# Summing gathered expert rows four tokens at a time instead of two, in a one-core layer with product-key experts

## The chip, the cores and the metric

The program runs on one core of one Trainium2 chip. The metric is the device time of one execution in microseconds (us), lower is better. The number to compare is the median over several executions.

## What is computed

One layer of a streaming encoder is applied to 1024 frames of a new stream (eight blocks of 128 tokens) and to 64 frames of a running one (a ninth block, called SAMPLE). Attention and retention come first and lead to `x1`; they matter here only as work that runs beside. The second half is a layer of 16384 single-neuron experts. Every token picks 128 of them (8 heads, 16 each) and computes

```
q = (xblk @ w_q).reshape(PEER_BLOCK, PEER_HEADS, 2, PEER_HALF)
...
u = u_table[expert]
hid = jax.nn.gelu(jnp.einsum('thkd,td->thk', u, xblk).astype(jnp.float32), approximate=False)
v = v_table[expert]
return jnp.einsum('thk,thkd->td', (g * hid).astype(xblk.dtype), v)
```

Both tables have rows of 1024 float32, so a token needs 128 rows of 4 KB from `u_table` and 128 from `v_table`. For 1088 tokens that is 1.14 GB of gathered rows.

## The kernel before

A **gather** is one indirect DMA of 128 rows (512 KB), issued by GpSimd (POOL in the profile) at L618. A u gather fetches one expert for each of the 128 tokens of a block; VectorE (DVE, L865) multiplies it with the tokens and adds up along the row. A v gather fetches the 128 experts of one token; TensorE (PE, L1195) sums them, weighted, into that token's row of the result. Both kinds land in one ring of `RING = 10` tiles, strictly in one order. POOL works through this order too: the gather that is number `n` waits until the tile of number `n - 10` has been read.

For the v tiles TensorE uses weights of 32 columns: `spread` holds, for each token, a 128x32 matrix with the token's weights in one column and zeros elsewhere. The product lands in one of four groups of 32 partitions of the accumulator, and `v_token` deals the tokens so that four successive v tiles go to the four groups in turn. A tile of 1024 columns takes two matmuls of 512 (`c` is 0 or 1), and a float32 matmul shows as two records in the profile. The v tiles are summed in pairs: the function `pair` waits for both tiles, issues four matmuls, and raises the semaphore `summed` once.

`seg_items` writes down the order. A segment `(u, v)` interleaves the u gathers of one block with the v gathers of an earlier one. After `LEAD = 8` u items come two v items, two u items, two v items and so on. Segment (8,7) has only 64 u gathers (the SAMPLE block is packed into half the slots), so there it is two v, one u. Segments (None,0) and (None,8) are v alone. The segments are grouped in `PHASES`; in each phase a pair of blocks goes through its dense work (projections, attention, output, query product, the search for the experts called the peer step). The class `Threader` places the ring items between the dense steps: before each dense step an engine first works off all items up to a slot that `Pace` gives. Each engine does this by itself in its program order, so a v item that TensorE has reached holds up its dense steps until the tiles have landed, and a u item does the same on VectorE. The last phase has no dense work: segments (7,6), (8,7) and (None,8).

The weights of the dense products come in pieces of 1 MB through the queue of SyncE (L501).

Of the kernel before, what the change touches and what calls it, by code (L numbers as in the profile page):

```python
# [27 lines left out]
P = 128  # L28
# [34 lines left out]
VBUF = 5  # L63
# [6 lines left out]
def rows(b):  # L70

    return CHUNK if b == SAMPLE else P


def u_slots(b):

    return SLOTS // 2 if b == SAMPLE else SLOTS


def u_before(b):  # L80
    return SLOTS * b


def v_before(b):
    return P * b


def v_token(b, i):

    groups = rows(b) // 32  # L90
    return 32 * (i % groups) + i // groups
# [14 lines left out]
def place(b):  # L106

    return 2 if b == 0 else next(blocks.index(b) for blocks, _ in PHASES if b in blocks)
# [4 lines left out]
    return [c for c in range(b + 1) if place(c) == place(b)]  # L113


PAIR = 2
LEAD = 8


def v_pairs(b):  # L120
    return rows(b) // PAIR


def pairs_before(b):
    return P * b // PAIR


def seg_items(prev, seg):


    u, v = seg
    us = [("u", u, k) for k in range(u_slots(u))] if u is not None else []
    vs = [("v", v, k) for k in range(rows(v))] if v is not None else []
    lead = LEAD if us else 0
    items = [("load", u, 0)] * bool(us) + us[:lead // 2]
    if prev[0] is not None:
        items.append(("spread", prev[0], 0))
    items += us[lead // 2:lead]
    if prev[1] is not None:
        items.append(("final", prev[1], 0))  # L140
    if not vs:
        return items + us[lead:] + [("weights", u, 0)]
    at, n = lead, len(vs) // PAIR
    for q in range(n):
        items += vs[PAIR * q:PAIR * q + PAIR]
        to = min(len(us), lead + -(-len(us) * (q + 1) // n))
        items += us[at:to]
        if us and at < len(us) == to:
            items.append(("weights", u, 0))
        at = max(at, to)  # L150
    return items


def plan():

    prev, out = (None, None), []
    for _, segs in PHASES:
        items = []
        for seg in segs:
            items += seg_items(prev, seg)  # L160
            prev = seg
        out.append(items)
    out[-1].append(("final", prev[1], 0))
    return out
# [83 lines left out]
def hymba_peer_program(nc, x_prompt, x_sample, cache_attn_k, cache_attn_v, state_ret, attn_norm_g, w_in,  # L248
# [24 lines left out]
    with ExitStack() as ctx:  # L273
# [3 lines left out]
        def sem(name):  # L277
            return ctx.enter_context(nc.semaphore(name))
# [149 lines left out]
        summed = sem("summed")  # L428
# [48 lines left out]
        def await_tile(eng, kind, n):  # L477

            at = order[kind, n]
            eng.wait_ge(landed[at % RING], 16 * (at // RING + 1))  # L480
            return ring[:, at % RING, :]

        def nothing(*_):
            pass
# [120 lines left out]
        @block.gpsimd  # L605
        def _(pool):
            pool.memset(spread[:], 0.0).then_inc(cleared, 1)
            pool.memset(weight[:], 0.0).then_inc(cleared, 1)
            pool.memset(state[:, :, :], 0.0).then_inc(cleared, 1)

            def gather(at, table, idx):
                if at >= RING:
                    kind, n = gathers[at - RING]
                    if kind == "u":
                        pool.wait_ge(dots_done, n + 1)
                    else:
                        pool.wait_ge(summed, n // PAIR + 1)
                pool.indirect_dma_start(ring[:, at % RING, :], None, table,  # L618
                                        bass.IndirectOffsetOnAxis(ap=idx, axis=0)).then_inc(landed[at % RING], 16)

            def item(kind, b, k):
                if kind == "u":
                    i, n = b % UBUF, u_before(b) + k
                    if b == 0 and k == 0:
                        pool.wait_ge(first_experts, 1)
                        pool.wait_ge(x1_stored[place(0)], 16)
                    if k == (SLOTS // 2 if b == 0 else 0):
                        pool.wait_ge(expert_ready, 2 * b + 1)
                        if b == SAMPLE:
                            pool.wait_ge(sample_packed, 48)  # L630
                    gather(order["u", n], u_table, u_idx[:, i, k:k + 1])
                elif kind == "v":
                    i, n, t = b % VBUF, v_before(b) + k, v_token(b, k)
                    if k == 0:
                        pool.wait_ge(expertT_ready, b + 1)
                    gather(order["v", n], v_table, v_idx[:, i, t:t + 1])

            th = Threader(item)
            for n_phase, (blocks, _) in enumerate(PHASES):
                th.phase(n_phase)  # L640
                th.rest()
# [202 lines left out]
        def _(dve):  # L844
# [40 lines left out]
            def spread_out(u):  # L885
                dve.wait_ge(weightT_ready, u + 1)
                if u:
                    dve.wait_ge(summed, pairs_before(u))
                if u != SAMPLE:
                    dst = spread[:].rearrange("p (j c) -> p j c", j=4)[:, :, 0:1024:33]  # L890
                    ch.put(v_.tensor_copy(dst, weightT[:].rearrange("p (j r) -> p j r", j=4)),
                           spread_ready)
                else:
                    for half in (slice(0, 64), slice(64, 128)):
                        dst = spread[half, 0:2048].rearrange("p (j c) -> p j c", j=2)[:, :, 0:1024:33]
                        w = v_.tensor_copy(dst, weightT[half, half].rearrange("p (j r) -> p j r", j=2))  # L896
                    ch.put(w, spread_ready)

            def final(v):
                T = rows(v)  # L900
                dve.wait_ge(summed, pairs_before(v) + v_pairs(v))
                dve.wait_ge(x1_in, 16 * (v + 1))
                acc = ps[0:T, B_ACC:B_ACC + 2, :].rearrange("p a n -> p (a n)")
                ch.put(v_.tensor_tensor(x1_v[0:T, :], x1_v[0:T, :], acc, ALU.add))  # L904
                ch.settle()
                ch.put(v_.tensor_tensor_reduce(out=acc, in0=x1_v[0:T, :], in1=x1_v[0:T, :], scale=1.0,  # L906
                                               scalar=0.0, op0=ALU.mult, op1=ALU.add,
                                               accum_out=fin_s[0:T, 0:1]), acc_read)
                ch.settle()
                ch.put(v_.tensor_scalar(fin_s[0:T, 1:2], fin_s[0:T, 0:1], 1.0 / D, EPS, ALU.mult, ALU.add), fin_ms)  # L910
                dve.wait_ge(fin_sd, v + 1)
                ch.put(v_.reciprocal(fin_s[0:T, 3:4], fin_s[0:T, 2:3]))  # L912
                ch.settle()
                ch.put(v_.scalar_tensor_tensor(out=x1_v[0:T, :], in0=x1_v[0:T, :], scalar=fin_s[0:T, 3:4],  # L914
                                               in1=g_fin[0:T, :], op0=ALU.mult, op1=ALU.mult), y_ready)
# [50 lines left out]
            for n_phase, (blocks, _) in enumerate(PHASES):  # L966
# [130 lines left out]
                for g, b in enumerate(blocks):  # L1097
# [16 lines left out]
                    for h0, h1 in ((0, PH // 2), (PH // 2, PH)) if b == 0 else ((0, PH),):  # L1114
# [4 lines left out]
                        pair = top_v[0:T, c0:c1, :].rearrange("p (h s) k -> p h s k", s=2)  # L1119
# [48 lines left out]
                    th.step("peer", g, 0.98)  # L1168
                    dve.wait_ge(expert_tr, b + 1)
                    if b >= VBUF:  # L1170
                        dve.wait_ge(summed, pairs_before(b - VBUF) + v_pairs(b - VBUF))
                    ch.put(v_.tensor_copy(v_idx[:, b % VBUF, 0:T], ps[:, 0, 0:T]), expertT_ready)
                th.rest()

# [1 line left out]
        @block.tensor  # L1176
        def _(pe):
            def item(kind, b, k):
                if kind == "v" and k % PAIR == PAIR - 1:
                    pair(b, k // PAIR)  # L1180
                elif kind == "weights":
                    pe.wait_ge(weight_ready, b + 1)
                    pe.transpose(ps[:, B_UX, 0:P], weight[:], ident).then_inc(weight_tr, 1)

            def pair(v, q):
                if q == 0:
                    pe.wait_ge(spread_ready, v + 1)
                    if v:
                        pe.wait_ge(acc_read, v)
                tokens = [v_token(v, PAIR * q + i) for i in range(PAIR)]  # L1190
                tiles = [await_tile(pe, "v", v_before(v) + PAIR * q + i) for i in range(PAIR)]
                for c in range(2):
                    for t, tile in zip(tokens, tiles):
                        j = 32 * (t // 32)
                        mm = pe.matmul(ps[j:j + 32, B_ACC + c, :], spread[:, 32 * t:32 * t + 32],  # L1195
                                       tile[:, 512 * c:512 * c + 512], start=(t % 32 == 0),
                                       stop=(t % 32 == 31), skip_group_check=True)
                mm.then_inc(summed, 1)
# [231 lines left out]
```

## Time and profile before

| | |
|---|---|
| median of three runs | 3459.91 us (3458.19 to 3460.81) |
| the profiled execution's own time | 3459.91 us |
| its span, first to last instruction | 3458.1 us |
| busy: TensorE matmul, VectorE, GpSimd, ScalarE | 68%, 59%, 61%, 9% |
| mean busy share of the 16 DMA engines | about 0.97, 372 GB/s |
| mean granted clock of TensorE | 0.842 of full speed |

Engines in rows: PE is TensorE's matmuls, PEld its weight loads, DVE is VectorE, ACT is ScalarE, POOL is GpSimd, SPq the queue of SyncE. L1195 is a line number of the kernel. A row of instructions gives their busy time and, behind the bar, the idle time of the engine just before them with what ended it. `x8` in a timeline counts records. The share of DMA engines reads slightly over 1 when all are busy, because packets overlap.

### The profile page before, as it was taken

The page shows a single profiled execution, that of the slowest core. Times are in us where ns is not written, and L with a number is a line of the kernel's source. Part 1 is how long each engine was busy: PE and PEld are TensorE (multiplying, and loading weights), DVE is VectorE, ACT ScalarE, POOL GpSimd, SP SyncE. Part 2 cuts the span into 40 slices and gives each one's busy share as a digit, 9 for nine tenths or more (in the row PEclk, how much of TensorE's full clock was granted, in tenths as well). Part 3 has the DMA queues.
Part 4 walks back from the last instruction along what each step waited for, and adds up shares of the span by engine and source line. Part 5 has one row for each costly group of instructions (what it writes and reads, how often), then busy time and mean ns, then how long its engine had stood idle before and what let it go on. Part 6 is the DMA issues. An engine that isn't in the chain of part 4 may idle for free. (4 is left out here: it accounts for less than half of the span.)

```text
span 3458.1 us, 27579 instructions
## 1 busy us (share of the span) xinstructions
PE 2339.7 (68%) x9448; PEld 1145.8 (33%) x9448; DVE 2037.9 (59%) x4581; ACT 308.7 (9%) x705; POOL 2110.0 (61%) x2183
## 2 busy tenths in 40 slices
PE   6985777774894559778955568768855555555556
PEld 6774632463561115434511124324411111111111
DVE  2389756569637883575467863664487944444320
ACT  2211010012100010110100010110100000000000
POOL 0045547745556775576567775575577777777765
PEclk9985899985898779888977789889977766688999
DMA  7597989998999999999999999999999999999998
GB/s 236 177 328 278 396 308 368 392 392 308 344 371 394 365 352 393 397 398 391 399 393 369 408 376 394 400 391 401 381 406 382 383 403 409 409 410 410 409 409 348
DMA packets 442170, 1286.15 MB, mean 372 GB/s; under 512 B 39408, under 2 KB 157936, under 8 KB 442032
## 3 DMA queue, kind: packets, MB, share of 16 engines
q0 software_dynamic: 313344, 1140.99, 84.8%
q1 hardware_dynamic: 126224, 134.48, 11.5%
q10 hardware_dynamic: 2464, 8.91, 0.7%
q8 instruction: 77, 1.26, 0.1%
q14 instruction: 61, 0.50, 0.0%
HBM read 1274.50 MB, written 9.44 MB: 371 GB/s over the span
## 5 line engine op out<-in xcount | busy, mean ns | idle before, releaser
L865 DVE CUSTOM_DVE_ANT_0 ring<-ring,ps 128x1024 f32<-128x1024 f32 x1088 | 1303.4, 1218 | 966.1 <-DMA ring<-in_peer_u_dram,u_idx 917.4
L1195 PE MATMUL ps<-ring,spread 128*32 128x512 f32 x4352 | 1283.1, 728 | 856.0 <-DMA ring<-in_peer_v_dram,v_idx 817.7
L618 POOL DMA_INDIRECT ring<-in_peer_u_dram,u_idx x1088 | 1050.7, 966 | 880.9 <-PE ps L1195 282.7
L618 POOL DMA_INDIRECT ring<-in_peer_v_dram,v_idx x1088 | 1054.9, 970 | 448.5 <-issue 266.6
L1195 PEld LDWEIGHTS ps<-ring,spread 128*32 128x32 f32 x4352 | 271.0, 122 | 1751.5 <-issue 1749.0
L1236 PE MATMUL ps<-wbuf,actT 128*128 128x256 f32 (+1 forms) x2944 | 699.6, 395 | 54.9 <-DMA wbuf<-in_w_in_dram 28.5
L1236 PEld LDWEIGHTS ps<-wbuf,actT 128*128 128x128 f32 (+1 forms) x2944 | 547.8, 190 | 249.7 <-issue 156.2
L952 DVE MAX8 work<-work 128x8 f32<-128x128 f32 (+3 forms) x432 | 110.2, 322 | 45.1 <-ACT work L832 43.4
L956 DVE FIND_INDEX8 work<-work 128x8 uint32<-128x128 f32 (+3 forms) x432 | 133.5, 329 | 0.0
L865 DVE DVE_READ_ACCUMULATOR2_ANT hidden<- 128x1 f32 x1088 | 89.3, 82 | 0.0
L1236 PE MATMUL ps<-wbuf,ring 128*128 128x256 f32 x368 | 84.8, 393 | 2.1 <-ACT ring L707 0.7
L1236 PEld LDWEIGHTS ps<-wbuf,ring 128*128 128x128 f32 x368 | 72.5, 198 | 13.6 <-ACT ring L796 1.1
L1203 PE MATMUL ps<-const,h_nat 128*128 128x128 f32 (+1 forms) x144 | 26.1, 343 | 64.1 <-DVE h_nat L1075 48.8
L722 ACT COPY wide<-ps 128x256 f32<-128x256 f32 x88 | 32.5, 371 | 409.7 <-PE ps L1236 390.4
L961 DVE MATCH_REPLACE8 work<-work 128x128 f32<-128x128 f32 (+3 forms) x216 | 66.4, 319 | 0.0
L904 DVE TENSOR_TENSOR x_v<-x_v,ps 128x1024 f32<-128x1024 f32 (+1 forms) x9 | 10.9, 1216 | 80.3 <-PE ps L1195 80.3
L658 ACT ACTIVATE hidden<-hidden 128x128 f32<-128x128 f32 (+1 forms) x9 | 2.7, 303 | 619.3 <-DVE hidden L865 619.3
L837 ACT ACTIVATE work<-work 128x128 f32<-128x128 f32 (+1 forms) x9 | 2.8, 309 | 614.8 <-DVE work L1133 614.8
L1086 DVE TENSOR_TENSOR x_in<-x_in,ps 128x256 f32<-128x256 f32 (+1 forms) x32 | 13.4, 420 | 73.6 <-PE ps L1236 73.6
L818 ACT COPY wide<-ps 128x256 f32<-128x256 f32 x64 | 23.8, 371 | 300.0 <-PE ps L1236 282.4
L1307 PE MATMUL ps<-state,work 128*128 128x128 f32 (+1 forms) x72 | 22.1, 400 | 39.5 <-issue 39.5
L1203 PEld LDWEIGHTS ps<-const,h_nat 128*128 128x128 f32 (+1 forms) x144 | 21.1, 182 | 73.6 <-DVE h_nat L1075 50.5
(153 smaller groups left out, 1274.3 us busy)
## 6 DMA issues: line engine op xcount, KB each, us to landing
wbuf<-in_w_in_dram SPq DMA_DIRECT2D x55, 1024.0 KB, 16.4
wbuf<-in_peer_w_q_dram SPq DMA_DIRECT2D x40, 1024.0 KB, 19.1
wbuf<-in_w_out_dram SPq DMA_DIRECT2D x20, 1024.0 KB, 17.5
ring<-in_peer_u_dram,u_idx POOLq DMA_INDIRECT x1088, 7.7
ring<-in_peer_v_dram,v_idx POOLq DMA_INDIRECT x1088, 7.9
x_v<-x_scratch ACTq DMA_DIRECT2D x8, 512.0 KB, 6.7
out_dram<-x_v ACTq DMA_DIRECT2D x8, 512.0 KB, 6.9
x_in<-in_x_prompt_dram SPq DMA_DIRECT2D x7, 512.0 KB, 10.6
```

The source lines that it names most:

```text
L618: pool.indirect_dma_start(ring[:, at % RING, :], None, table, bass.IndirectOffsetOnAxis(ap=idx, axis=0)).then_inc(landed[at % RING], 16)
L722: ch.put(copy(dst, src), proj_ready)
L818: ch.put(copy(pq_of[b][0:rows(b), p * WCOLS:(p + 1) * WCOLS], ps[0:rows(b), 2 + m % 2, 0:WCOLS]), q_ready)
L865: ch.put(v_.tensor_tensor_reduce(out=row, in0=row, in1=ux_ps, scale=1.0, scalar=0.0, op0=ALU.mult, op1=ALU.add, accum_out=hidden[:, k:k + ...
L952: ch.put(v_.max(best[0:T, c, out], values[0:T, c, :]))
L956: ch.put(v_.max_index(where[0:T, c, out], best[0:T, c, out], values[0:T, c, :]))
L961: ch.put(v_.match_replace(values[0:T, c, :], best[0:T, c, out], values[0:T, c, :], -3.0e38))
L1086: ch.put(v_.tensor_tensor(x, x, ps[0:T, 2 + m % 2, 0:WCOLS], ALU.add), x1_ready)
L1195: mm = pe.matmul(ps[j:j + 32, B_ACC + c, :], spread[:, 32 * t:32 * t + 32], tile[:, 512 * c:512 * c + 512], start=(t % 32 == 0), stop=(t % ...
L1203: mm = pe.transpose(ps[0:width, bank, c * P:c * P + T], src(c), ident[0:T, 0:T])
L1236: mm = pe.matmul(ps[0:T, 2 + m % 2, 0:WCOLS], act_of[b][:, k, 0:T], wbuf[:, n % WRING, k, :], start=(k == 0), stop=(k == KC - 1))
L1307: pe.matmul(ps[0:T, 2, a * P:(a + 1) * P], qrTs[:, a, 0:T], state[:, a, :], start=True, stop=False, skip_group_check=True)
```

## The change

The v tiles are summed four at a time. `PAIR = 2` becomes `QUAD = 4`; the function `pair` becomes `quad`, which waits for four tiles and then issues the four matmuls of `c = 0` (one for each group of 32 columns) and the four of `c = 1`, and raises `summed` once. All waits on `summed` count in quads. The same constant stands in `seg_items`, so the order of the ring changes as well: four v items, four u items, four v items and so on; in segment (8,7) four v, two u. `RING`, `LEAD`, the number of gathers, of matmuls and of dots stay as they are.

```
-PAIR = 2
+QUAD = 4
 LEAD = 8
...
-def v_pairs(b):
-    return rows(b) // PAIR
+def v_quads(b):
+    return rows(b) // QUAD
...
-    at, n = lead, len(vs) // PAIR
+    at, n = lead, len(vs) // QUAD
     for q in range(n):
-        items += vs[PAIR * q:PAIR * q + PAIR]
+        items += vs[QUAD * q:QUAD * q + QUAD]
         to = min(len(us), lead + -(-len(us) * (q + 1) // n))
         items += us[at:to]
...
                     if kind == "u":
                         pool.wait_ge(dots_done, n + 1)
                     else:
-                        pool.wait_ge(summed, n // PAIR + 1)
+                        pool.wait_ge(summed, n // QUAD + 1)
...
             def item(kind, b, k):
-                if kind == "v" and k % PAIR == PAIR - 1:
-                    pair(b, k // PAIR)
+                if kind == "v" and k % QUAD == QUAD - 1:
+                    quad(b, k // QUAD)
...
-                tokens = [v_token(v, PAIR * q + i) for i in range(PAIR)]
-                tiles = [await_tile(pe, "v", v_before(v) + PAIR * q + i) for i in range(PAIR)]
+                tokens = [v_token(v, QUAD * q + i) for i in range(QUAD)]
+                tiles = [await_tile(pe, "v", v_before(v) + QUAD * q + i) for i in range(QUAD)]
```

The waits on `summed` at L888, L901 and L1171 are rewritten in the same way, with the same meaning.

## Rows read from the trace of the kernel before

**Rows 1.** The page: engines, and the queues' share of DMA time

```profile
PE 2339.7 (68%) x9448; PEld 1145.8 (33%) x9448; DVE 2037.9 (59%) x4581; ACT 308.7 (9%) x705; POOL 2110.0 (61%) x2183
...
q0 software_dynamic: 313344, 1140.99, 84.8%
q1 hardware_dynamic: 126224, 134.48, 11.5%
```

**Rows 2.** Windows: length, busy per engine, then clock, DMA share, GB/s

```profile
440.00:480.00 40.00, 28.16 (x159) 20.76 (x157) 8.04 (x50) 9.39 (x17) 4.68 (x5) 0.96 0.57 195
780.00:900.00 120.00, 59.00 (x258) 50.77 (x260) 115.03 (x206) 25.38 (x64) 64.32 (x69) 0.54 0.81 298
1020.00:1040.00 20.00, 18.73 (x90) 12.87 (x88) 5.28 (x9) 3.52 (x8) 11.24 (x12) 1.00 0.83 286
1060.00:1300.00 240.00, 131.97 (x423) 37.27 (x421) 208.34 (x588) 14.20 (x26) 170.27 (x165) 0.76 0.97 369
1300.00:1420.00 120.00, 109.16 (x478) 68.36 (x474) 43.11 (x71) 7.82 (x21) 69.08 (x74) 1.00 1.04 393
1740.00:2060.00 320.00, 175.65 (x546) 44.71 (x545) 248.97 (x664) 14.21 (x28) 230.47 (x229) 0.74 1.00 386
2500.00:2770.00 270.00, 143.62 (x446) 33.01 (x448) 221.91 (x619) 5.42 (x11) 201.85 (x203) 0.79 1.00 385
2790.00:3110.00 320.00, 179.88 (x495) 35.47 (x497) 156.18 (x255) 4.36 (x6) 233.45 (x248) 0.72 1.03 409
3113.00:3358.00 245.00, 126.81 (x502) 29.58 (x501) 83.16 (x138) 3.29 (x5) 178.59 (x191) 0.94 1.03 409
```

**Rows 3.** Waits of the whole span: total us, times, longest

```profile
POOL ring L618 <- PE ps L1195: 372.6, 249, 41.0
...
POOL ring L618 <- DVE hidden L865: 279.6, 290, 18.6
```

**Rows 4.** Timeline of the last phase, one turn of two v and two u

```profile
2901.08 3.62 PE L1195 MATMUL ps<-ring,spread 128*32 128x512 f32 x8 [2.15 <-DMA ring<-in_peer_v_dram,v_idx]
...
2904.97 0.94 POOL L618 DMA_INDIRECT ring<-in_peer_u_dram,u_idx  x1 [0.77 <-PE ps L1195]
...
2906.20 3.62 PE L1195 MATMUL ps<-ring,spread 128*32 128x512 f32 x8 [1.50 <-DMA ring<-in_peer_v_dram,v_idx]
2906.22 0.94 POOL L618 DMA_INDIRECT ring<-in_peer_u_dram,u_idx  x1 [0.30 <-issue]
...
2911.32 1.91 PE L1195 MATMUL ps<-ring,spread 128*32 128x512 f32 x8 [1.50 <-DMA ring<-in_peer_v_dram,v_idx]
```

**Rows 5.** Timeline of five pairs in one go, and the gather behind them

```profile
471.77 5.34 PE L1195 MATMUL ps<-ring,spread 128*32 128x512 f32 x40
...
473.97 0.94 POOL L618 DMA_INDIRECT ring<-in_peer_v_dram,v_idx  x1 [40.99 <-PE ps L1195]
```

**Rows 6.** DMA view, 2767 to 3000 us: gathers, median us from issue to landing

```profile
ring<-in_peer_u_dram,u_idx POOLq DMA_INDIRECT x90, 7.6
ring<-in_peer_v_dram,v_idx POOLq DMA_INDIRECT x89, 7.7
```

**Rows 7.** Timeline of a gather after a pause

```profile
300.70 0.94 POOL L618 DMA_INDIRECT ring<-in_peer_u_dram,u_idx  x1 [5.46 <-DVE hidden L865]
```

**Rows 8.** DMA view, 300 to 310 us, in 40 slices

```profile
GB/s 0 0 0 0 0 0 0 0 0 197 115 66 131 344 393 410 361 262 344 295 279 328 311 344 328 410 328 377 295 295 393 246 328 262 295 410 377 426 344 410
...
ring<-in_peer_u_dram,u_idx POOLq DMA_INDIRECT x7, 5.4
```

**Rows 9.** POOL's u gathers by line between 1230 and 1262 us

```profile
L618 POOL DMA_INDIRECT ring<-in_peer_u_dram,u_idx x8 | 13.3, 1666 | 2.4 <-issue 2.4
```

**Rows 10.** Timeline of a pair in a dense stretch, and the product behind it

```profile
1312.09 1.91 PE L1195 MATMUL ps<-ring,spread 128*32 128x512 f32 x8
...
1313.93 3.72 PE L1236 MATMUL ps<-wbuf,actT 128*128 128x256 f32 x16
```

More of the change, by code:

```diff
@@ L113, in sharing, with quads_before @@
     return [c for c in range(b + 1) if place(c) == place(b)]
-PAIR = 2
+QUAD = 4
 LEAD = 8
-def v_pairs(b):
-    return rows(b) // PAIR
-def pairs_before(b):
-    return P * b // PAIR
+def v_quads(b):
+    return rows(b) // QUAD
+def quads_before(b):
+    return P * b // QUAD
 def seg_items(prev, seg):
@@ L887, in spread_out @@
                 if u:
-                    dve.wait_ge(summed, pairs_before(u))
+                    dve.wait_ge(summed, quads_before(u))
                 if u != SAMPLE:
@@ L900, in final @@
                 T = rows(v)
-                dve.wait_ge(summed, pairs_before(v) + v_pairs(v))
+                dve.wait_ge(summed, quads_before(v) + v_quads(v))
                 dve.wait_ge(x1_in, 16 * (v + 1))
@@ L1170, in _ @@
                     if b >= VBUF:
-                        dve.wait_ge(summed, pairs_before(b - VBUF) + v_pairs(b - VBUF))
+                        dve.wait_ge(summed, quads_before(b - VBUF) + v_quads(b - VBUF))
                     ch.put(v_.tensor_copy(v_idx[:, b % VBUF, 0:T], ps[:, 0, 0:T]), expertT_ready)
@@ L1183, in item, with quad @@
                     pe.transpose(ps[:, B_UX, 0:P], weight[:], ident).then_inc(weight_tr, 1)
-            def pair(v, q):
+            def quad(v, q):
                 if q == 0:
```

## The prediction

> **What bounds the kernel now.** I read the page first. No engine is busy more than 68% of the span, while the two big DMA queues together take 96.3% of the time of all 16 DMA engines [rows 1]. Then I cut the span into windows, to see where those engines are full and where they are not [rows 2]. The reader should look at the last two columns. With gathers alone a full queue moves 409 GB/s at a share of 1.03; with weights beside them it is 393 GB/s at 1.04. Idle DMA time sits in few places. 440 to 480 us is the start of the first v segment. In 780 to 900 us VectorE is busy for 115 of 120 us. In the three stretches of the peer steps (1060 to 1300, 1740 to 2060, 2500 to 2770) VectorE is busy 78 to 87% of the time, and the share is 0.97 to 1.00. The dense stretch 1300 to 1420 has TensorE busy 109 of 120 us and still a full DMA share. So before asking whether TensorE gets faster, one must ask what keeps the DMA queue full. That is the ring of ten: POOL waits 372.6 us in all for TensorE to give back v tiles and 279.6 us for VectorE [rows 3]. Most of these waits cost nothing, because several gathers are under way meanwhile.
>
> **How tight the ring is.** In the last phase a turn of four gathers takes 5.12 us (the pairs start at 2901.08 and 2906.20), so a gather is due every 1.28 us; POOL needs 0.94 + 0.30 = 1.24 us for one [rows 4]. POOL can hardly catch up what it loses. Ten tiles are worth 12.8 us. A tile of a pair is held for 1.28 us until its partner lands, then 3.62 us for the matmuls at the lower clock (2.0 us at the higher), then about 0.3 us until POOL runs. 12.8 - 1.28 - 3.62 - 0.3 = 7.6 us is left for the gather itself, and 7.6 and 7.7 us is what the DMA view shows from issue to landing [rows 6]. The sum closes, so I use it for the quad.
>
> How short may that time become before the queue runs dry? After a pause, with nothing ahead of it, a gather issued at 300.70 us starts to move data in the slice at 302.25, and the seven gathers of that window take 5.4 us at the median [rows 7, 8]. I take 5.4 us as the least a gather needs.
>
> **The change, part by part.**
>
> *The matmuls.* Their number and size stay (1088 tiles, two each). What changes is how many column groups run side by side. A pair lasts 1.91 us at the full clock and 3.62 at the half [rows 4]: four passes one behind the other in each of two groups. Five pairs in one go, which fall on all four groups, take 5.34 us, so a further pair costs (5.34 - 1.91) / 4 = 0.86 us and not 1.91 [rows 5]. Four groups do run side by side. A quad has the same four passes per group, so I take 1.91 plus some 0.2 us for starting two more groups, 2.1 us, and 3.62 plus 0.25, about 3.85 us, at the half clock. Both ends are bounded: below by a pair's 1.91, above by two pairs after each other, 3.8 and 7.2. TensorE's time for v tiles falls by almost half. A dense product has to wait for the pair to end (1312.09 to 1313.93, that is 1.84 us) [rows 10]; two pairs cost 3.7 us there, a quad 2.1. So eight ring items free 1.6 us of TensorE in the dense stretches. I count this at nothing where the DMA share is 1.03 or 1.04, because the DMA queue is the cover. It counts where TensorE holds the ring and the DMA share is low: 1020 to 1040 us, where 0.20 of 20 us, or 4 us, is idle [rows 2]. With a few short places like it I put the gain at 5 us, between 0 and 15.
>
> *The 41 us wait of POOL* at 432 to 474 us ends with the first pair [rows 5]. TensorE reaches it only after dense work, and all ten tiles have landed by then. A quad there ends 0.1 to 0.2 us later. Nothing is gained.
>
> *The ring.* The first tile of a quad waits for three more, 3.84 us instead of 1.28, and is then held for the quad. What is left for a gather is 12.8 - 3.84 - 0.3 - Q = 8.66 - Q: 6.5 us at the full clock and 4.8 us at the half. The latter is below the 5.4 us that a gather needs. Put as a loop: with four v and four u in turn, the third tile of a quad goes into the place of the first tile of the quad before. From the end of one quad to the end of the next there are 0.3 us until POOL runs, 1.24 us for one gather, 5.4 us for the next from issue to landing, 0.1 us to start, and Q. That is 7.0 + Q, against 8 x 1.28 = 10.24 us that DMA needs. At Q = 2.1 the loop takes 9.1 us and is hidden. At Q = 3.85 it takes 10.85 us, and 0.6 us of DMA time are lost per quad. The point at which it decides is Q = 3.24. For the pair the same loop runs over three turns (15.36 us) and takes 0.3 + 3 x 1.24 + 5.4 + 0.1 + 3.62 = 13.1 us; it has 2.2 us to spare.
>
> *The clock.* So it hangs on the clock a quad meets. In the last phase 495 records, 62 pairs, took 179.9 us, 2.9 us each, at a mean clock of 0.72 with TensorE busy 56% [rows 2]. A cold pair (3.62 of 5.12 us busy) was followed by another and then by one at 2.4 GHz [rows 4]. In segment (8,7), a pair each 3.84 us, the clock is 0.94. With quads TensorE is busy 2 to 4 us and then has 6 to 8 us with nothing, where now the gaps are 1.5 to 2.2 us [rows 4], so I expect it to be at 1.2 GHz at nearly every start, and to rise inside some of the quads. Between 2.1 and 3.85 I take 3.6 us, near the cold end. *TensorE: Matmul & The Clock Gate*, section "HAM oscillation — how this bites in real kernels", of the Trainium skill says that waits for DMA between short bursts of matmuls bring the clock down each time; by that rule all quads are cold, Q is 3.85, the loss is 0.6 us for each of 112 quads, and the sum below would be 3525 us. The trace agrees as far as it goes, with 0.72 in this phase.
>
> *The sum.* Loss per quad 7.0 + 3.6 - 10.24 = 0.36 us. Segment (7,6) without dense work: 320 / 10.24 = 31 quads, 11 us. The three stretches of peer steps: 830 / 10.24 = 81 quads, 29 us; there POOL's gathers are now and then slower too (1.67 instead of 0.94 us) [rows 9], which comes on top in the loop but is in part already a loss today, so I leave the number. Segment (8,7): a loop spans two turns, 0.3 + 5 x 1.24 + 5.4 + 0.1 + 3.6 = 15.6 us against 15.36, 0.1 per quad, 3 us for 32. Segment (None,8), a quad each 5.12 us: 7.0 + 3.6 against two turns of 5.12, but TensorE is then busy more than half the time and warmer; nothing. Dense stretches: eight gathers take 120 / 74 x 8 = 13 us beside the weights [rows 2]; the loop of 10.6 us leaves 2.4 us for the product that a quad may find in its way; nothing. Together 43 us lost and 5 gained, +38: 3459.9 + 38 = 3498 us. The profiled execution is the median of the three runs; its span plus 1.8 us is its time, so nothing has to be scaled.
>
> *The dots.* VectorE now gets four u tiles in a row, 1.28 us apart, and a dot takes 1.22 + 0.08 us. It keeps up; cost nothing while VectorE has time. In the peer stretches it has not, and then its hold adds to POOL's lead as now. `spread`, `final` and the copy of `v_idx` wait for the same last tile as before.
>
> **The rivals.**
> - *The ring stays loose* (no change): the quads run warm, or a gather behind a short queue lands sooner than 5.4 us. Q below 3.24 us, or a gather in at most 5.0 us at Q = 3.6, is enough. Then 3459.9 - 5 + 0 to 5 gives 3457 us. For it speaks that the average pair today is 2.9 us. The Trainium skill, *DMA: Bandwidth & Descriptors*, section "Anatomy of one DMA — SWDGE (gpsimd) path", gives 2.0 us plus the bytes at 436 GB/s, an estimate of 3.2 us for 512 KB. By that page the loop would take 8.4 us at Q = 3.6 and nothing would be lost. The row says 5.4 us, and I follow the row.
> - *Faster*: TensorE is what holds the dense stretches. The place is 900 to 1060, 1300 to 1420 and their two like. POOL's waits for TensorE there are 2 to 8 us long, and 1.6 us less per eight items would shorten them. It decides from the point where more than half of those waits have no full DMA queue behind them. The share of 1.04 speaks against it. Upper end of the gain, 15 us: 3445 us.
> - *Much slower*: in the peer stretches the loop also takes POOL's slow gathers (two of them, 0.7 us more each) and VectorE's late dots, 1 us a quad instead of 0.36, and all quads are cold (0.6): 81 x 1.2 + 31 x 0.6 + 32 x 0.25 = 124 us: 3580 us; half of it, 3520 to 3550, is likelier.
> - *The change doesn't do what it says*: the four groups don't run side by side within a quad, because the matmuls are issued in another order than in five pairs. Q is then 3.8 to 7.2, the loop 11 to 14 us, and 144 quads lose 2 us or more: over 3740 us. The 5.34 us speaks against it [rows 5].
>
> **How the numbers follow.** My forecast has a chance of 0.50, with a range of its own of 3468 to 3525. The loose ring 0.20, faster 0.12, much slower 0.15, the groups not side by side 0.03. The range for 8 in 10 goes from 3452 us, into the loose ring, to 3550. A difference of 0.2%, 7 us, is about what a measurement of this kernel can tell from no change. Slower is 0.50 + 0.15 + 0.03 and a little of the loose ring, 0.70; same is 0.18; faster 0.12.
>
> **What the profile after would show.** A quad of 16 records in 1.9 to 2.3 us at the full clock and 3.6 to 4.1 at the half; if 3.8 and 7.2, the last rival is right. In 2790 to 3110 us a DMA share below 1.03 and a turn of more than 10.24 us, the gathers landing in 5 to 6.5 us instead of 7.7, and a clock nearer to 0.5 than 0.72. If the share there stays 1.03, the loop is loose and the prediction is wrong there. In 1300 to 1420 us TensorE below 100 of 120 us busy at the same share. A dense stretch that gets shorter would refute the zero I gave it.

## The result and the profile after

The change makes the kernel slower: 3583.54 us median (3582.41 to 3590.06, four runs) against 3460.36 (3458.19 to 3460.89, four runs); ratio 1.0362, interval 1.0343 to 1.0379. The direction was forecast; 3498 us was not, and 3583.5 lies outside the range of 3452 to 3550.

Page of the changed kernel: the engines, the clock in 40 slices, the big queues. They answer to [rows 1].

```profile
span 3593.1 us, 27579 instructions
...
PE 1974.5 (55%) x9448; PEld 1081.0 (30%) x9448; DVE 2040.1 (57%) x4581; ACT 309.6 (9%) x705; POOL 2120.9 (59%) x2183
...
PEclk8986887885886578778756588688755555556668
...
q0 software_dynamic: 313344, 1140.99, 83.8%
q1 hardware_dynamic: 126224, 134.48, 11.1%
```

TensorE does the same records in 365 us less busy time, and the kernel is 123 us slower. Windows of the changed kernel in the places of [rows 2] (length, busy PE, PEld, DVE, ACT, POOL, then clock, DMA share, GB/s):

```profile
780.00:900.00 120.00, 57.74 (x280) 52.15 (x279) 108.28 (x194) 28.23 (x68) 60.50 (x64) 0.61 0.88 325
1020.00:1040.00 20.00, 18.39 (x93) 14.41 (x92) 4.92 (x8) 1.49 (x4) 12.09 (x13) 1.00 1.04 393
1060.00:1300.00 240.00, 79.48 (x380) 21.87 (x381) 200.32 (x585) 13.14 (x23) 164.01 (x161) 0.59 0.96 357
1300.00:1420.00 120.00, 95.84 (x452) 65.40 (x452) 49.35 (x81) 7.98 (x21) 69.92 (x74) 0.88 1.03 396
1740.00:2060.00 320.00, 115.03 (x577) 38.77 (x577) 234.01 (x637) 13.20 (x23) 213.56 (x212) 0.62 0.98 364
2870.00:3180.00 310.00, 98.98 (x444) 18.62 (x436) 137.53 (x224) 1.28 (x1) 208.24 (x222) 0.58 0.99 377
3240.00:3480.00 240.00, 103.02 (x469) 20.07 (x473) 65.31 (x109) 1.80 (x3) 162.30 (x173) 0.64 0.99 377
3490.00:3580.00 90.00, 64.25 (x228) 16.98 (x226) 0.00 (x0) 0.00 (x0) 50.70 (x54) 0.82 0.91 331
```

The dense window 1300 to 1420 keeps its DMA rate with TensorE at 96 instead of 109 us. In segments (7,6) and (8,7) the rate has gone from 409 to 377 GB/s and TensorE's clock from 0.72 and 0.94 to 0.58 and 0.64; in the last segment the rate has gone from 382 (3370 to 3450 us before) to 331. The first v segment has lost the higher clock too: 0.97 in 480 to 640 us before, 0.72 in 480 to 660 now.

To see where the time goes I read from the timelines when each block's last output operation (DVE, L914) starts, and take the differences. In the last phase these are the segments (7,6), (8,7) and (None,8). The table has the kernel before, the changed one and the experiments below; all are profiled executions, that of the changed kernel 3594.93 us long, 11 us above its median.

| us | block 0 | to 1 | to 2 | to 3 | to 4 | to 5 | to 6: (7,6) | to 7: (8,7) | to 8: (None,8) |
|---|---|---|---|---|---|---|---|---|---|
| before | 659.6 | 633.2 | 393.3 | 364.4 | 394.0 | 353.3 | 330.7 | 240.1 | 84.8 |
| changed | 674.9 | 632.6 | 401.1 | 386.9 | 395.7 | 376.7 | 358.0 | 261.1 | 101.6 |
| order_only | 661.4 | 642.6 | 400.4 | 361.3 | 397.6 | 353.7 | 330.4 | 240.3 | 84.9 |
| group_only | 672.0 | 681.9 | 459.6 | 444.1 | 451.8 | 439.0 | 436.8 | 286.0 | 98.0 |
| quad_ring12 | 662.6 | 628.8 | 386.0 | 364.3 | 387.4 | 351.2 | 331.5 | 240.3 | 88.6 |
| pair_ring12 | 657.5 | 624.9 | 388.0 | 358.7 | 391.1 | 345.9 | 331.6 | 239.8 | 84.8 |
| pair_ring8 | 670.3 | 647.6 | 407.6 | 388.2 | 415.2 | 384.0 | 354.8 | 244.3 | 86.3 |
| quad_warm | 675.1 | 635.7 | 400.2 | 384.5 | 398.5 | 378.4 | 334.5 | 241.3 | 94.7 |
| quad_sample_pairs | 676.5 | 634.8 | 397.0 | 383.9 | 396.5 | 375.7 | 357.9 | 261.4 | 85.6 |
| single | 662.1 | 656.3 | 425.4 | 375.9 | 425.1 | 369.2 | 330.1 | 240.7 | 84.7 |
| pair_ring12_w2 | 722.2 | 648.3 | 401.5 | 370.1 | 406.7 | 353.2 | 330.9 | 240.0 | 84.3 |
| quad_ring12_w2 | 719.6 | 657.9 | 401.9 | 364.4 | 399.9 | 356.8 | 331.2 | 240.3 | 88.9 |

The 135 us of the changed kernel's profiled execution are: 15 in the stretch to block 0, which holds the first v segment; 23 and 23 in those to block 3 and to block 5, which hold the second and the third stretch of peer steps; 8 in the one to block 2, which has dense work and no peer step; 27, 21 and 17 in the three segments of the last phase; and 1 in the other two. The first stretch of peer steps (1060 to 1300 us) lies in the one to block 1, which as a whole is 0.6 us shorter.

Timeline of the changed kernel in segment (7,6), one turn:

```profile
3050.99 3.64 PE L1195 MATMUL ps<-ring,spread 128*32 128x512 f32 x16 [7.78 <-DMA ring<-in_peer_v_dram,v_idx]
...
3054.92 0.94 POOL L618 DMA_INDIRECT ring<-in_peer_v_dram,v_idx  x1 [1.78 <-PE ps L1195]
...
3056.16 0.94 POOL L618 DMA_INDIRECT ring<-in_peer_v_dram,v_idx  x1 [0.30 <-issue]
3057.40 0.94 POOL L618 DMA_INDIRECT ring<-in_peer_u_dram,u_idx  x1 [0.30 <-issue]
...
3062.41 3.44 PE L1195 MATMUL ps<-ring,spread 128*32 128x512 f32 x16 [7.78 <-DMA ring<-in_peer_v_dram,v_idx]
```

This is the loop of the prediction, link by link. The quad ends at 3054.63, POOL starts the third v gather 0.29 us later and the fourth after 1.24 us more, at 3056.16; the next quad starts at 3062.41, 6.25 us behind it. The turn is 11.42 us where DMA needs 10.24. Two things stand there that the prediction had: a quad of 16 records takes 3.64 us, as long as a cold pair of 8 [rows 4], and between two quads TensorE is idle for 7.8 us. The third link is longer than forecast, 6.25 us and not 5.4 + 0.1. The DMA view of 2870 to 3180 us says the same (median us from issue to landing; [rows 6] had 7.6 and 7.7):

```profile
ring<-in_peer_v_dram,v_idx POOLq DMA_INDIRECT x112, 6.1
ring<-in_peer_u_dram,u_idx POOLq DMA_INDIRECT x110, 6.2
```

and the DMA view of one turn, 3051 to 3063 us in 40 slices of 0.3 us, shows the rate falling behind POOL's pause:

```profile
GB/s 410 437 396 382 410 423 410 437 410 410 396 382 410 423 410 437 410 437 369 341 273 287 341 437 396 314 328 328 369 314 328 328 259 341 246 232 232 232 300 314
```

From the nineteenth slice on the rate is 232 to 369 GB/s, but for two slices. Over the whole segment some 4.4 gathers are under way at a time (6.2 us each, one in 310 / 222 = 1.40 us), where it was 6.0 before (7.7 us each, one in 1.28 us).

How long a gather takes grows with how many are ahead of it. The DMA view of single gathers shows it: in the kernel before, the one issued at 300.70 us, after the pause of [rows 7] and with nothing under way, and the one issued at 304.43, the fourth behind that pause; in the changed kernel the one issued at 3054.92, the first behind POOL's pause, with two still under way.

```profile
ring<-in_peer_u_dram,u_idx POOLq DMA_INDIRECT x1, 4.2
ring<-in_peer_u_dram,u_idx POOLq DMA_INDIRECT x1, 5.9
ring<-in_peer_v_dram,v_idx POOLq DMA_INDIRECT x1, 4.8
```

The gather that the quad waits for is the next one, and it is not as quick: the quad starts 6.25 us after its issue. What holds the later ones up inside the queue is not shown by any run.

### The profile page after: what moved, and what is told of

It is laid out like the page before. It is cut to its first block, busy times and chain, and to the rows that moved or that the text cites. A ratio compares the mean times of both kernels' runs of the same rounds, so it can differ in the third digit from the quotient of the medians.

```text
span 3593.1 us, 27579 instructions
## 1 busy us (share of the span) xinstructions
PE 1974.5 (55%) x9448; PEld 1081.0 (30%) x9448; DVE 2040.1 (57%) x4581; ACT 309.6 (9%) x705; POOL 2120.9 (59%) x2183
## 3 DMA queue, kind: packets, MB, share of 16 engines
q1 hardware_dynamic: 126224, 134.48, 11.1%
## 4 chain that ended last, share of the span: by engine, by line
DMA 35%; PE 21%; POOL 9%; DVE 5%; issue 5%; ACT 0%; POOLq 0%; ACTq 0%; DVEq 0%
DMA ring<-in_peer_v_dram,v_idx 30%; PE ps L1195 17%; POOL ring L618 9%; PE ps L1236 3%; DMA wbuf<-in_peer_w_q_dram 2%; DVE ring L865 2%; DMA ring<-in_peer_u_dram,u_idx 2%; DVE work L956 1%; PE ps L1394 0%; DMA wbuf<-in_w_out_dram 0%; DVE work L1143 0%; DVE work L1148 0%; DVE work L1150 0%; DVE work L952 0%; PE ps L1203 0%
## 5 line engine op out<-in xcount | busy, mean ns | idle before, releaser
L1195 PE MATMUL ps<-ring,spread 128*32 128x512 f32 x4352 | 893.4, 930 | 1299.2 <-DMA ring<-in_peer_v_dram,v_idx 1295.8
L618 POOL DMA_INDIRECT ring<-in_peer_v_dram,v_idx x1088 | 1067.5, 981 | 773.7 <-PE ps L1195 479.2
L1195 PEld LDWEIGHTS ps<-ring,spread 128*32 128x32 f32 x4352 | 181.3, 145 | 1904.0 <-issue 1903.2
L1236 PEld LDWEIGHTS ps<-wbuf,actT 128*128 128x128 f32 (+1 forms) x2944 | 562.4, 195 | 255.0 <-issue 154.7
L1236 PE MATMUL ps<-wbuf,ring 128*128 128x256 f32 x368 | 84.9, 394 | 2.1 <-ACT ring L707 0.7
```

What stands on the lines that cost most here:

```text
L1236: mm = pe.matmul(ps[0:T, 2 + m % 2, 0:WCOLS], act_of[b][:, k, 0:T], wbuf[:, n % WRING, k, :], start=(k == 0), stop=(k == KC - 1))
```

## The experiments

**order_only.** The order of the ring as in the changed kernel, TensorE in pairs.

```
-    at, n = lead, len(vs) // PAIR
+    at, n = lead, len(vs) // 4
...
-        items += vs[PAIR * q:PAIR * q + PAIR]
+        items += vs[4 * q:4 * q + 4]
```

> The ring takes four v, four u in turn as in the changed kernel, but TensorE still waits for, sums and releases two tiles at a time. Theory A (the loss is the longer hold of v tiles by the grouping on TensorE): no tight loop remains, total within 5 us of before, 3455 to 3466 us. Rival B (the loss comes from the order: four dots in a row and four v gathers in a row): 3520 us or more, up to the 3584 of the changed kernel.

3477.57 us, ratio 1.0040 (1.0024 to 1.0056). The order alone costs 0.4% and not 3.6%. The last phase and the stretches to block 3 and 5 are as before, within 3 us; the 19 us of its profiled execution sit in the stretches to block 1, 2 and 4, by 9, 7 and 4 us. The bound of 3466 us was missed by 12 us, and what the order does there was not tried. The prediction had no term for the order beside the dots.

**group_only.** The order of before, TensorE in quads.

```
-        items += vs[QUAD * q:QUAD * q + QUAD]
+        items += vs[2 * q:2 * q + 2]
```

(and `len(vs) // 2` in the line above it.)

> The ring keeps two v, two u in turn, but TensorE sums four v tiles at once, so a quad spans six ring places. Theory A: from the end of a quad to the last landing of the next there are 0.3 + 4 issues of 1.24 + 6.2 + 0.1 and 3.6 us for the quad, about 14 to 15 us for eight gathers where DMA needs 10.24: segment (7,6) takes about 440 to 470 us instead of 331, the total is 3900 to 4150 us. Rival B (the order is what costs): close to before, below 3500 us.

3975.59 us in one run. Its PE timeline shows a quad each 13.5 us (the window ends at 3318 us and cuts the second one off after four records):

```profile
3303.94 3.57 PE L1195 MATMUL ps<-ring,spread 128*32 128x512 f32 x16 [9.88 <-DMA ring<-in_peer_v_dram,v_idx]
3317.43 1.08 PE L1195 MATMUL ps<-ring,spread 128*32 128x512 f32 x4 [9.92 <-DMA ring<-in_peer_v_dram,v_idx]
```

Here the last tile of a quad comes three issues behind the first that is freed (the expectation had counted four): 0.3 + 3.72 + 6.2 + 0.1 + 3.6 = 13.9 us. The segment took 436.8 / 32 = 13.7 us per eight gathers, a little less than the 440 to 470 us expected. Grouping on TensorE is what costs, and the more so the wider the group lies in the ring.

**quad_ring12 and pair_ring12.** Changed kernel and kernel before with twelve tiles.

```
-RING = 10
+RING = 12
...
-        g_ffn = sb("g_ffn", [P, D])
-        g_fin = sb("g_fin", [P, D])
+        g_ffn = g_fin = g_attn
...
```

Both leave out the loads of the second and third gain vectors and use the first in their place; without that there is no room for the tiles. Their outputs differ for it, and the experts that a token picks can too; the number and size of the gathers are the same.

> The changed kernel with a ring of twelve tiles. To make room, the gains of the second and the last norm are those of the first (two loads of 512 KB less at the start). Theory A (the ring is too short for the hold): two more tiles are 2.56 us of lead, the loop of a quad no longer closes within a turn, and the no-dense segments return to a DMA share of 1.03: 3450 to 3480 us in all, the rest being the last segment. Rival C (the lower clock of TensorE itself costs the time, whatever the ring): over 3540 us.

> The kernel before with the same ring of twelve and the same gains, as the control of quad_ring12. Theory A: the queue is already full outside the peer steps, a longer lead helps only while VectorE slows POOL or holds u tiles: 3435 to 3460 us. Rival C says the same; it is a control, and a value above 3465 would say that the room made has a cost of its own.

3444.38 us, ratio 0.9947 (0.9930 to 0.9964), and 3429.94 us, ratio 0.9906 (0.9881 to 0.9932). Both lie below what was expected, by 6 and 5 us. Two tiles more take 139 us from the changed kernel and 32 us from the one before (against the 3461.58 us measured beside it), so 14 us are left between quads and pairs. What the two omitted loads give by themselves was not tried; the stretch to block 0, where they lie, is 2 us shorter in pair_ring12. Window of quad_ring12 in segment (7,6), and its gathers there:

```profile
2860.00:3150.00 290.00, 103.79 (x465) 19.96 (x465) 136.80 (x223) 4.36 (x6) 210.51 (x224) 0.66 1.03 409
```

```profile
ring<-in_peer_v_dram,v_idx POOLq DMA_INDIRECT x116, 7.7
ring<-in_peer_u_dram,u_idx POOLq DMA_INDIRECT x108, 7.5
```

The quads are still mostly cold (clock 0.66, 3.6 us each), and the segment is back at 331.5 us. In this segment the lower clock by itself costs nothing; it costs when the ring has no tile to spare.

**pair_ring8.** The kernel before with `RING = 8`.

> The kernel before with a ring of eight tiles. Theory A: holding two more tiles is the same as having two fewer. A pair is released, 0.3 us, two gathers issued (1.24 us apart), 6.2 us, 0.1 us, next pair but one 3.0 to 3.6 us: 10.8 to 11.5 us for two turns of 10.24 in all, the same loop as the quad's. Segment (7,6) 348 to 365 us, total 3540 to 3620 us, near the changed kernel. Rival B (the order or the form of the quad costs, not the number of free tiles): below 3500 us.

3601.75 us, ratio 1.0407 (1.0374 to 1.0440). PE timeline:

```profile
3100.77 3.45 PE L1195 MATMUL ps<-ring,spread 128*32 128x512 f32 x8 [3.62 <-DMA ring<-in_peer_v_dram,v_idx]
3106.78 3.14 PE L1195 MATMUL ps<-ring,spread 128*32 128x512 f32 x8 [2.56 <-DMA ring<-in_peer_v_dram,v_idx]
```

Two tiles fewer under pairs do nearly what quads do under ten: 354.8 us for (7,6) against 358.0, with the pair, its order and its clock (0.71) as before. The expected total, near that of the changed kernel, came out, but (7,6) is where the two are alike; that the totals lie so near each other is in part chance. The stretches to block 1 and 4 are 14 and 21 us longer than before, where those of the changed kernel are 0.6 us shorter and 1.7 us longer, and segment (8,7) hardly suffers (244.3 us, against 261.1).

**quad_warm.** The changed kernel with extra matmuls in the last phase, whose results nobody reads.

```
                 if kind == "v" and k % QUAD == QUAD - 1:
                     quad(b, k // QUAD)
+                elif last[0] and kind in ("u", "v"):
+                    await_tile(pe, kind, (u_before(b) if kind == "u" else v_before(b)) + k)
+                    pe.matmul(ps[:, 0, 0:384], ident, const[:, 384:768], start=True, stop=True)
...
```

`last[0]` is set when the last phase begins.

> The changed kernel; in the last phase TensorE also runs one float32 matmul of 384 columns, whose result nobody reads, after each landed tile that doesn't complete a quad. It keeps the clock up. Theory A (loop of 7.8 us plus the quad, 3.6 us when cold): a warm quad of 1.9 to 2.1 us makes the loop 9.9 us, below the 10.24 of DMA, so segment (7,6) goes from 358 us back to 330 to 336 us and (8,7) from 261 to 243 to 250; together 35 to 45 us less than the changed kernel, 3540 to 3550. Rival D (the wait for four tiles costs whatever the clock): (7,6) stays above 350 us.

3544.6 us in two runs (3539.62 and 3549.58), ratio 1.0232 (1.0209 to 1.0256). Window of (7,6), and of the quads alone in it:

```profile
2860.00:3150.00 290.00, 221.11 (x821) 72.31 (x820) 142.74 (x234) 1.49 (x2) 209.64 (x223) 0.99 1.02 405
```

```profile
2860.00:3150.00 290.00, 53.45 (x432) 13.63 (x432) 0.99 1.02 405
```

27 quads took 53.45 us, 1.98 us each, the loop is 0.3 + 1.24 + 6.2 + 0.1 + 2.0 = 9.8 us, and the segment falls from 358.0 to 334.5 us, (8,7) from 261.1 to 241.3. The gathers now land after 6.8 and 6.7 us (v and u). More work on TensorE made the kernel 39 us faster. So in these two segments, with ten tiles, it is the cold clock that tips the balance, as the prediction had it; in the stretches before them the quads were not warmed.

**quad_sample_pairs.** The changed kernel, block SAMPLE in pairs (`size(b)` is 2 for SAMPLE and 4 otherwise, in the order, in `quad` and in the counts of `summed`).

> The changed kernel, but the 64 tokens of the SAMPLE block are summed in pairs, and ordered so. For this block v_token uses two column groups only, so its quad runs eight passes in a row: 3.6 us warm and 7.2 cold. Theory: the last segment returns from 101.6 us to 84 to 87 us, the rest stays: 3566 to 3572 us. Rival (the last segment loses by the same hold as the others): less than 5 us, above 3577.

3567.43 us, ratio 1.0294 (1.0277 to 1.0311), 16 us below the changed kernel, all in the last segment (101.6 to 85.6 us). The PE timeline of the changed kernel shows what this removes:

```profile
3552.08 3.63 PE L1195 MATMUL ps<-ring,spread 128*32 128x512 f32 x16 [3.68 <-DMA ring<-in_peer_v_dram,v_idx]
3557.46 3.63 PE L1195 MATMUL ps<-ring,spread 128*32 128x512 f32 x16 [1.76 <-DMA ring<-in_peer_v_dram,v_idx]
3563.17 8.86 PE L1195 MATMUL ps<-ring,spread 128*32 128x512 f32 x32 [2.08 <-DMA ring<-in_peer_v_dram,v_idx]
3575.50 9.76 PE L1195 MATMUL ps<-ring,spread 128*32 128x512 f32 x32 [3.47 <-DMA ring<-in_peer_v_dram,v_idx]
```

`v_token` deals the 64 tokens of this block to `rows(b) // 32`, that is two column groups, not four (the description ahead of the prediction said four for all). Its quad runs eight passes in a row: 3.63 us at the full clock, as long as a cold quad of the other blocks. Two of them in one go take 8.86 and 9.76 us, where two warm ones would take 7.3.

**single.** The kernel before with `PAIR = 1`.

> The kernel before with PAIR = 1: each v tile is summed and released by itself, and the order is v, u, v, u. Theory A: a tile waits for no partner, 1.28 us more lead than the pair, so the queue is full wherever it is now and a little better in the peer steps: 3445 to 3462 us. The risk it names: TensorE pays 1.84 us for each tile before a dense product, 7.4 us per eight ring items instead of 3.7, and the dense stretches, where it is 91% busy, become bound by it: then 3500 to 3650 us.

3572.93 us, ratio 1.0309 (1.0292 to 1.0326). The named risk came true. PE timeline of a dense stretch:

```profile
1351.91 1.91 PE L1195 MATMUL ps<-ring,spread 128*32 128x512 f32 x4
1353.75 1.99 PE L1236 MATMUL ps<-wbuf,actT 128*128 128x256 f32 x8
1355.67 1.90 PE L1195 MATMUL ps<-ring,spread 128*32 128x512 f32 x4
1357.51 1.99 PE L1236 MATMUL ps<-wbuf,actT 128*128 128x256 f32 x8
```

A single tile costs TensorE as much as a pair or a full quad, 1.9 us. Between 1318 and 1744 us TensorE is busy 394.6 of 426 us, 220.0 of them with v tiles; in the kernel before it was 321.1 of 393.3, 143.2 with v tiles. The stretches to blocks 1, 2 and 4 are 23, 32 and 31 us longer, those to 3 and 5 12 and 16, while the last phase is as before, its gathers landing after 10.6 us at the median and its clock 1.00 (2930 to 3230 us).

**pair_ring12_w2 and quad_ring12_w2.** A ring of twelve with all gains in place; the room comes from `WRING = 2` instead of 3.

> The kernel before with a ring of twelve tiles, the room taken from the weight pieces (two places instead of three); nothing else changes. Theory A: more lead for the gathers gives what pair_ring12 gave, about 30 us, unless the products now wait for their pieces: a piece lands some 16 to 19 us after its issue and two products of a pair of blocks last 22 us beside the gathers, so most of the wait is hidden. 3430 to 3450 us. If the weights become the bound: over 3480 us.

> The changed kernel with the same ring of twelve and two places for weights. Theory A: 12 to 18 us over pair_ring12_w2, as quad_ring12 stood to pair_ring12, and below the kernel before: 3442 to 3465 us. The place of the difference is the peer steps and the last segment.

3565.06 us, ratio 1.0294 (1.0275 to 1.0312), and 3567.50 us, ratio 1.0293 (1.0274 to 1.0312). Both miss their expectation by over 100 us, and the quads' is 2 us above the pairs', not 12 to 18. Block 0 ends at 722.2 instead of 659.6 us in the profiled execution of pair_ring12_w2. Its waits between 0 and 340 us, before any v gather:

```profile
POOL ring L618 <- DVE u_idx L1156: 204.4, 1, 204.4
...
PE ps L1236 <- DMA wbuf<-in_w_in_dram: 30.6, 8, 10.0
```

TensorE waits 30.6 us for weight pieces (1.6 us before), and POOL gets its first list of experts 30 us later than before (204.4 instead of 174.3 us). The rest of the 62 us was not followed. The other stretches to block 4 lose 6 to 15 us each. The third place for weights is worth more than two more tiles in the ring; no version with all its gains that beats the kernel before was found.

## Why the prediction was right and wrong, step by step

*Right: the loop is the mechanism.* The sum of 0.3 us, one issue of 1.24, a gather and the quad, against 10.24 us of DMA, is the one that the timeline shows, with 6.2 us for the gather. The signs named for it came out too: in (7,6) a DMA share of 0.99 instead of 1.03, gathers that land in 6.1 and 6.2 us, a clock of 0.58. The 6.2 us is read from that segment itself; in group_only (with one issue too many), pair_ring8 and quad_warm the loop was worked out with it before they ran:

| case | loop worked out | measured per eight gathers |
|---|---|---|
| changed, (7,6) | 7.84 + 3.6 = 11.4 | 358.0 / 32 = 11.2 |
| changed, (8,7), two turns | 0.3 + 6.2 + 6.2 + 0.1 + 3.6 = 16.4 | twelve gathers: 16.7 (the 26 quads between 3240 and 3460 us start 8.36 us apart) |
| group_only, (7,6) | 13.9 | 13.7 |
| pair_ring8, (7,6), Q 3.0 | 10.8 | 354.8 / 32 = 11.1 |
| quad_warm, (7,6), Q 2.0 | 9.8, so DMA sets it | 334.5 / 32 = 10.5 |
| before, (7,6) | three turns, spare | 330.7 / 32 = 10.3 |

*Right: the matmuls.* Four column groups run side by side; 3.64 us cold, 1.92 us warm (the 2.1 forecast was a little high).

*Right: the clock.* Forecast 3.6 us a quad; measured 98.98 us for 444 records, 27.75 quads, 3.57 us each, at 0.58. *TensorE: Matmul & The Clock Gate* of the Trainium skill, section "HAM oscillation — how this bites in real kernels", agrees with this row.

The forecast, stretch by stretch, against what the profiled execution shows. To measure a stretch I took when POOL issues the same gather, counted in the order of the ring, in both kernels, and how much that lag grows over the stretch (times are those of the kernel before; the lag is 1 us at 440). Its numbers differ by up to 2 us from those by block ends:

| us | forecast | changed | order_only |
|---|---|---|---|
| 440 to 660, first v segment | no term | 17 | -1 |
| 660 to 966 | 0 | -5 | 2 |
| 966 to 1060, with the short place at 1020 | -4 | -3 | 0 |
| the three stretches of peer steps | 29 | 45 (4, 19, 22) | 8 |
| dense, 1300 to 1740 and 2060 to 2500 | 0 | 16 (11, 4) | 8 |
| segment (7,6) | 11 | 27 | 0 |
| segment (8,7) | 3 | 20 | 1 |
| segment (None,8) | 0 | 18 | -1 |

The same measure in quad_warm and quad_sample_pairs, where they don't differ from the changed kernel, agrees within 1 us in 440 to 660 and within 4 us in each of the other rows.

*Wrong: "I take 5.4 us as the least a gather needs".* This is the step that failed. 5.4 us is no least: it is the median over the seven gathers of a window in which they take between 4.2 us, for the first after the pause, and 5.9 us. In the loop the gather that counts starts behind others, and the medians of (7,6) are 6.1 and 6.2 us. The term 7.0 + Q is 7.84 + Q, the loss per quad 1.2 by the formula and 27.3 / 32 = 0.85 as the segment has it, against 0.36. In (7,6) 11 us became 27. The three stretches of peer steps took 45 us instead of 29; 1.2 us for each of 81 quads would be 97, so there the formula gives too much, and why was not followed. The point at which the clock decides moves from Q = 3.24 to 2.4 us. The rival that a gather behind a short queue lands sooner is refuted for this loop. So is, as the time for it, the estimate of 3.2 us from *DMA: Bandwidth & Descriptors* of the Trainium skill, section "Anatomy of one DMA — SWDGE (gpsimd) path". It comes near only with an empty queue: the 4.2 us at 300.70 are counted from the start of POOL's instruction and hold its 0.94 us, so 3.3 us are left.

*Wrong: no loss in the segments of v alone.* The first, (None,0), has no term in the sum at all. There the same loop spans two turns and gives (7.84 + 3.6 - 10.24) / 2 = 0.6 us a quad, 19 us for 32; the stretch to block 0 lost 15. For the last I argued that TensorE would be warmer, and missed that SAMPLE uses two column groups. That cost 17 us, and quad_sample_pairs gives 16 of them back.

*Wrong in size: segment (8,7).* With 6.2 us the loop is 16.4 us against 15.36, 0.5 us a quad, and 3 us become 17; it lost 21.

*Half right: the zero for the dense stretches.* TensorE's time fell from 109 to 96 of 120 us and nothing was gained by it, as forecast. But the dense stretches lost 16 us; order_only loses 8 in them, so a part may be the order's, and the rest was not followed. The 4 us of 1020 to 1040 did appear: the share went from 0.83 to 1.04, and between 966 and 1030 us all three kernels with this ring and quads gain 5 to 6 us.

*The rivals.* "Much slower" named 3580 us and the total came there, but not by its account: it put 97 us into the peer steps, which took 45, and 27 into the last phase, which took 65. That its total comes so near is chance. "The groups not side by side" holds for one block of nine.

## What to carry to other kernels

A batch of n tiles that are waited for and freed together takes n - 1 tiles out of the ring while it fills. Before widening it, write down the loop from a free tile through issue, landing and use to the next free tile, and compare it with the time the transfers need; a busy DMA queue today says nothing about the margin. Take the latency in this sum from gathers with as many ahead of them as the loop leaves, and not from the first ones after a pause; look for every segment in which the loop runs, and check a grouping for the blocks that are smaller than the rest.

## What the runs showed of the hardware that was not expected

- The DMA engines' busy share hardly shows a starved queue: 0.99 at 377 GB/s in (7,6) of the changed kernel, 1.03 at 409 before. GB/s is the column to read.
- Added matmuls without use made a kernel faster by 39 us: with them TensorE's granted clock was 0.99 instead of 0.58 where its bursts lay in the loop of the ring, and a quad took 1.98 instead of 3.57 us.
- A gather of 512 KB landed after 4.2 us with nothing ahead of it, after 5.9 us as the fourth behind a pause, after 6.2 us in the median with some 4.4 under way, and after 7.7 us in a full queue.
- One tile in one column group, a pair in two and a quad in four take the same 1.9 us at the full clock; a dense product behind them waits 1.84 us for a single tile as for a pair.
